# First group: low parts of the product, branch and output weights made by VectorE, those of the plain blocks by GpSimd

## The reference, cut to what matters

```
p = rms_norm(x, norm_gain) @ w_in          # columns: aq ak av ag | bq bf bi bg | ma mb
attn_o = window attention with sinks (aq, ak, av), window of two chunks of 64 tokens
rec_o  = gated linear recurrence (bq, f = lb + (1-lb)*sigmoid(bf), bi), state per head 128 x 128
ya = (attn_o * silu(ag)) @ w_branch_a
yb = (rms_norm per head(rec_o) * silu(bg)) @ w_branch_b
merged = sigmoid(ma) * ya + sigmoid(mb) * yb
y = rms_norm(x + merged @ w_out, final_norm_gain)
```

## Time and profile before

| | |
|---|---|
| runs, median (lowest to highest) | 1585.51 us (1581.87 to 1587.05), 3 runs |
| profiled execution | 1583.75 us, span 1581.8 us |
| mean granted TensorE clock | 0.989 |
| busy: PE, VectorE, ScalarE, GpSimd | 1519.4, 959.8, 537.4, 228.6 us |

### The profile page before, as it was taken

One profiled execution on the slowest core, in us unless ns is written; L12 is line 12 of the kernel. 1 busy time (PEld: TensorE's weight loads), 2 busy tenths in 40 slices (PEclk: granted clock), 3 DMA queues, 4 the chain that ended last, 5 costly groups with the idle time before them and its releaser, 6 DMA issues.

```text
span 1581.8 us, 24395 instructions
## 1 busy us (share of the span) xinstructions
PE 1519.4 (96%) x9727; PEld 1464.4 (93%) x9727; DVE 959.8 (61%) x1543; ACT 537.4 (34%) x1161; POOL 228.6 (14%) x155
## 2 busy tenths in 40 slices
PE   6999999988999799999999999999999999999996
PEld 5999899978999799999999999999989999999996
DVE  5558776973476854567777126675566758513624
ACT  5345553333413422555223110232256422210022
POOL 1422224256643400000100000100000010000000
PEclk9999999999999999999999999999999999999998
DMA  4743334378796464222226885536322233786352
GB/s 157 279 148 143 120 139 155 130 266 303 284 348 241 173 218 155 107 107 88 93 104 212 275 275 206 193 119 221 138 83 97 97 107 114 250 270 212 133 207 74
DMA packets 99136, 278.44 MB, mean 176 GB/s; under 512 B 11984, under 2 KB 29136, under 8 KB 99024
## 3 DMA queue, kind: packets, MB, share of 16 engines
q1 hardware_dynamic: 73968, 202.68, 37.6%
q10 hardware_dynamic: 25056, 74.20, 12.1%
HBM read 194.01 MB, written 82.84 MB: 175 GB/s over the span
## 4 chain that ended last, share of the span: by engine, by line
PE 81%; DVE 12%; DMA 2%; ACT 2%; issue 2%; POOL 1%; DVEq 0%; ACTq 0%
PE bank L1299 24%; PE bank L1301 23%; PE bank L1300 23%; DVE x_raw L954 2%; DMA raw<-in_w 2%; PE bank L1504 2%; PE bank L1430 1%; PE bank L1448 1%; PE bank L1500 1%; POOL w_unit L610 1%; PE bank L1486 1%; PE bank L1462 1%; PE bank L1472 1%; DVE x_acc L942 1%; PE bank L1439 1%
## 5 line engine op out<-in xcount | busy, mean ns | idle before, releaser
L1299 PE MATMUL bank<-x_hi,w_unit 128*128 128x320 f32 (+2 forms) x1680 | 556.3, 331 | 22.1 <-DVE sig L1230 9.8
L1301 PE MATMUL bank<-x_hi,w_unit 128*128 128x320 f32 (+2 forms) x1680 | 545.2, 325 | 0.0
L1300 PE MATMUL bank<-x_lo,w_unit 128*128 128x320 f32 (+2 forms) x1680 | 545.0, 324 | 0.0
L1299 PEld LDWEIGHTS bank<-x_hi,w_unit 128*128 128x128 f32 x1680 | 319.0, 190 | 33.4 <-issue 18.0
L1300 PEld LDWEIGHTS bank<-x_lo,w_unit 128*128 128x128 f32 x1680 | 319.3, 190 | 0.4
L1301 PEld LDWEIGHTS bank<-x_hi,w_unit 128*128 128x128 f32 x1680 | 318.7, 190 | 0.0
L610 POOL TENSOR_TENSOR w_unit<-w_raw,w_unit 128x512 fp32r<-128x512 f32 x102 | 145.2, 1442 | 295.4 <-ACT w_unit L657 275.4
L1299 PE MATMUL bank<-m_hi,w_unit 128*128 128x384 f32 (+1 forms) x384 | 126.3, 329 | 10.2 <-POOL w_unit L610 6.4
L1300 PE MATMUL bank<-m_lo,w_unit 128*128 128x384 f32 (+1 forms) x384 | 124.4, 324 | 0.0
L1301 PE MATMUL bank<-m_hi,w_unit 128*128 128x384 f32 (+1 forms) x384 | 124.4, 324 | 0.0
L1299 PEld LDWEIGHTS bank<-m_hi,w_unit 128*128 128x128 f32 x384 | 72.6, 189 | 13.1 <-issue 6.9
(11 more groups left out here) (206 smaller groups left out, 2608.8 us busy)
## 6 DMA issues: line engine op xcount, KB each, us to landing
w_unit<-w_parts SPq DMA_DIRECT2D x274, 512.0 KB, 4.2
w_parts<-w_unit ACTq DMA_DIRECT2D x137, 512.0 KB, 4.0
w_raw<-in_w SPq DMA_DIRECT2D x88, 256.0 KB, 3.6
res<-in_x_t SPq DMA_DIRECT2D x12, 704.0 KB, 6.9
raw<-in_w SPq DMA_DIRECT2D x28, 256.0 KB, 3.7
x_raw<-in_x_t SPq DMA_DIRECT2D x12, 384.0 KB, 8.6
out_y<-res SPq DMA_DIRECT2D x12, 384.0 KB, 5.9
x_raw<-in_x_t SPq DMA_DIRECT2D x12, 320.0 KB, 6.1
```

The source lines that it names most:

```text
L1299: pe.matmul(out, w_h, m_h, start=first, stop=False, **more)
L1300: pe.matmul(out, w_h, m_l, start=False, stop=False, **more)
L1301: return pe.matmul(out, w_l, m_h, start=False, stop=last_of_bank, **more)
```

## The change

GpSimd makes the low parts of the 56 plain units only. The other 81 are made by VectorE, from the unit `LOW_FROM` on, at places in the list of steps that a new function gives: `lows_after(step)` names the units whose low part follows a step, and they are put in behind it for group 0. In the products it is the unit four ahead, after each `prod`; ScalarE's stores go one unit further behind the high parts in the products.

```diff
--- before.py
+++ after.py
@@ -77,6 +77,7 @@
 NAMES = ([(b, i) for b in range(NP) for i in range(2)] + [(o, 0) for o in OPS]
          + [(b, i) for b in range(NP + len(MIXED), NB) for i in range(2)])
 UNITS = len(NAMES)
+LOW_FROM = 2 * NP
 PART = {n: u for u, n in enumerate(NAMES)}
 
 
@@ -114,6 +115,30 @@
 X_ALL = [step for n in X_STEPS for step in X_STEPS[n]]
 OUT = ([(j, s) for j in range(KT // 2) for s in range(2)] + [(j, s) for s in range(2) for j in range(KT // 2, KT)])
 SQUARES = len(OUT) - 2
+
+
+def lows_after(step):
+
+    kind, a, s = step
+    if kind == "evac":
+        b = BLOCK[a] + 2
+        late = a in ("av", "bf0")
+        names = [(b, i) for i in range(2) if (s == 1 if late else i == s)] if FIRST <= b < NP else []
+        names += {("ma0", 1): [(OPS[0], 0), (OPS[1], 0)], ("ma1", 1): [(OPS[2], 0), (OPS[3], 0)]}.get((a, s), [])
+    elif step == ("t_low", 3, 0):
+        names = [(OPS[4], 0)]
+    elif kind == "prod":
+        names = [(OPS[a + 4], 0)] if 1 <= a < NO - 4 else []
+        names += [(BLOCK["wab0"], i) for i in range(2) if a == NO - 2]
+    elif kind == "refill":
+        names = [(BLOCK["wab1"], i) for i in range(2)]
+    elif (kind, s) in (("ya", 1), ("yb", 0)):
+        names = [(BLOCK[f"wab{a}"] + 2, int(kind == "yb"))]
+    elif kind == "out" and a < MERGES - 2:
+        names = [(BLOCK[f"wo{a}"] + 2, i) for i in range(2) if (i == s if a < KT // 2 else s == 0)]
+    else:
+        names = []
+    return [PART[n] for n in names if PART[n] >= LOW_FROM]
 
 
 def steps(g):
@@ -191,6 +216,8 @@
             out += [("y_sum", 0, g), ("y_back", 0, g)]
     if last:
         out += [("y_sum", 1, g), ("y_back", 1, g)]
+    if g == 0:
+        out = [t for step in out for t in [step] + [("low", u, 0) for u in lows_after(step)]]
     return out
 
 
@@ -606,8 +633,8 @@
 
             u = 0, name, i
             pool.wait_ge(w_high, PART[name, i] + 1)
-            source = op_source(OP[name]) if name in OP else w_raw[PLACE[u]][:]
-            pool.tensor_tensor(low_of(u), source, high_of(u).bitcast(F32), ALU.subtract).then_inc(w_split, 1)
+            pool.tensor_tensor(low_of(u), w_raw[PLACE[u]][:], high_of(u).bitcast(F32),
+                               ALU.subtract).then_inc(w_split, 1)
 
         def x_back(dst, k, t):
 
@@ -617,7 +644,7 @@
 
         def body(g, last):
             for u, name in enumerate(NAMES):
-                if g == 0 and u >= 2 * FIRST:
+                if g == 0 and 2 * FIRST <= u < LOW_FROM:
                     low(*name)
                 if name == (BLOCK["ag0"], 1):
                     wait_read(pool, g, last, ("attend", NCH - 1, 0), 6)
@@ -665,7 +692,7 @@
             else:
                 act.wait_ge(s_made, 4 * p + (1 if op == "s3" else 4))
             act.activation(high_of((0, OPS[n], 0)), op_source(n), ACT.Copy).then_inc(w_high, 1)
-            keep_to(PART[OPS[n], 0] - 2)
+            keep_to(PART[OPS[n], 0] - 3)
 
         def prepare_x(step, g, gn, last):
             kind, s, _ = step
@@ -869,6 +896,7 @@
                 elif kind == "fetch":
                     if g == 0:
                         high(BLOCK[f"wab{a}"])
+                        keep_to(PART[BLOCK[f"wab{a}"], 0] - 2)
                 elif kind == "prod":
                     op, p = OPS[a]
                     bank = bank_of(g, step)
@@ -980,6 +1008,16 @@
             prepare_x(step, None, 0, False)
         dve.wait_ge(consts_in, 16 * 8)
         link(dve.tensor_scalar(neg_sink[:], sink[:], -1.0, None, ALU.mult))
+
+        def low(n):
+
+            name, i = NAMES[n]
+            u = 0, name, i
+            if n == LOW_FROM:
+                dve.wait_ge(w_split, LOW_FROM)
+            dve.wait_ge(w_high, n + 1)
+            source = op_source(OP[name]) if name in OP else w_raw[PLACE[u]][:]
+            dve.tensor_tensor(low_of(u), source, high_of(u).bitcast(F32), ALU.subtract).then_inc(w_split, 1)
 
         def split(hi, lo, val):
 
@@ -1240,6 +1278,8 @@
                         take(sig[:, br, j + 1, HT:T], v_sum[:], "s1")
                     else:
                         take(sig[:, br, j, HT:T], u, "s4")
+                elif kind == "low":
+                    low(a)
                 elif kind == "refill" and not last:
 
                     wait_op_done(dve, g, last, NO - 1)
```

## The result

The changed kernel takes 1586.54 us (median of 20 runs, 1584.79 to 1590.59), the kernel before 1584.47 us in the same comparison (20 runs). The ratio of the times is 1.0019, 95% interval 1.0013 to 1.0025: **slower by 2 to 4 us**, inside the 0.3% that was called no change. The forecast was 1582.1, 3.4 us under before: wrong in sign. The profiled execution of the changed kernel took 1585.42 us, 1.1 under its median, that of the kernel before 1583.75. A few executions, of whatever kernel, took 2600 to 5900 us and are left out of every time here.

A forecast was written before the change was run, and what follows sets the result against it. PE, busy 96%, was taken as the bound, so only its waits could pay. Gate products with opening -1.6 and output stage -1.8 gave -3.4 us, applied to the median 1585.51: 1582.1, range 1575.5 to 1588.5.

The forecast's parts named there:

- the two places named: PE waits in the gate products' pairs, about 10 us lost over five, and in the output stage at wo6 and wo7.
- the stretched neighbours: VectorE's two-input SBUF subtractions in the pairs, 1.57 and 1.66 us beside GpSimd, were to take 0.61 to 0.69 us.
- Opening, +3.7: Before s4 of pair 0: s1's low part stands behind `finish` on VectorE, so s4 starts about 340.6 against 336.93.
- The ring, -5.3 for five pairs: Gate products: the chain of stores, loads and parts repeating each pair was to take 14.6 us, against 15.66 before.
- the first leg: In each pair, from s2's to s4's high part, waiting for the store of a12: 4.13 us.
- the load's leg: In each pair, the load of the upper half of raw_1, up to a12's high part: 3.64 us.
- the stores and loads slow down: Rival for the pairs: same bytes in less time, store 4.5, load 4.1, ring 15.6, total 1587.0 us; chance 0.16.
- the slower rival: In the pairs, a12's late low part holds the take of s1: 16.6 us each, total 1592.0; chance 0.08.
- the last leg: In each pair, from a12's high part to the next s2's high part: 5.39 us.
- Branch projections, nothing: 16 low parts there add 0.61 us each to VectorE, hidden by PE's busy time of 7.7 us per block.
- my own signs of being wrong: s4 of pair 0 not later, period under 14 or over 15.3, or PE waiting in the branch projections.
- Output stage, -1.8: Group 0's output stage: with VectorE's work undisturbed, wo7's low part is ready at 543.6, where PE started at 545.45.

The follow-up runs named there:

- take first: The changed kernel with the low part of each pair's a12 behind the take of the pair's before s1 product, instead of ahead: 1584.85 us, ratio to before 1.0009.
- store early: The changed kernel with each product's high part again followed by the store of the unit two before it, not three: 1586.56 us, ratio to before 1.0019.
- half stores: The changed kernel with stores of the product units, and their loads in later groups, cut to the high half: 1576.59 us, ratio to before 0.9957.
- branch later: The changed kernel with the low parts of the branch projections' weights each behind a later take: 1585.78 us, ratio to before 1.0014.
- output only: The kernel before with only the low parts of the output projection's weights on VectorE, one more store at the first fetch: ratio to before 0.9993.

## Why the prediction was wrong

- **What bounds, and the prices.** Right: PE waits in the two places named, a low part costs VectorE 0.61 to 0.69 us, and the stretched neighbours went back to 0.69 (multiplications of the output stage 3.18 to 1.15).
- **Opening, +3.7.** Right in sign and mechanism, too large: +2.2. Measured from the common event the low part of s1 started at 29.35, forecast 29.4 (332.3 - 302.93). The load behind it was seen landed 2.6 us after its issue (330.61 on SP, then L1243 at 333.20), where I had taken 4.2; that is the difference. Leaving these low parts with GpSimd gives 1.4 of it back, and 1.9 to 2.1 with the take first. PE stood 4.21 us at s1 and not 6.
- **The ring, -5.3 for five pairs (-1.6 with the opening).** This is the step that failed, and with it the sign: the landing times of the transfers on the ring, above all the first leg, "store of a12: 0.03 + 4.0 to land", in all 4.13 us from s2's to s4's high part. It took 5.22 in the mean (5.64 in the pair shown), and the load's leg 3.95 for 3.64; all other legs together came 0.2 under the forecast. The 4.0 was no bad reading: a store at this place took 4.0 us before (356.90) and takes 5.5 now (355.41), with two raw loads issued 0.8 and 0.5 us ahead of it (354.57 and 354.94; before 1.8 and 0.7). The error was to carry the landing times of before into another order of transfers. Taking the same store out earlier moved the microsecond to the load (store early), and halving the bytes took 1.6 us off each pair (half stores). The rival "the stores and loads slow down" had it: a ring of 15.6, measured 15.8. I gave it 0.16, arguing that the stores would come spread out. They did (355.41 to 361.05 above, against four in 3.3 us), and that didn't help.
- **The take behind a12's low part**, the place of the slower rival, is real too, but small: 0.2 us a pair in the last leg, 0.8 to 2.8 us from s4 to s4 over the section, not 8.
- **Branch projections, nothing.** Wrong: "PE's busy time hides them" counted VectorE's work and left out that it works in order. A low part whose weights land late held a take for 5.6 us; PE waited 1.9, and the stretch from s4 of pair 6 to the first wait of the output stage took 94.42 us for 91.68 (91.85 in "branch later"). A wait of PE there was among my own signs of being wrong. This was the same head-of-line wait that I had priced for the pairs.
- **Output stage, -1.8.** Right in mechanism, and near in size: -1.5, in every kernel with these low parts on VectorE. It came mostly from the take of `res` (PE's idle behind it 1.73 to 0.68), less from wo6's own low part (4.78 to 4.42). The times of "output only" can't confirm it.

The losses of 2.2, 0.7 and 2.7, less 1.5, are the 4.2 us between the traces; that the runs show 3.0 is within what single profiles differ by. That the measured time lies in the range 1575.5 to 1588.5 comes from the range being wide: the terms of the forecast's sum missed by -1.5, +6.0, +2.7 and +0.3. What stays open is why two raw loads and two stores close together land later at the same share of the DMA engines, and how the clock's fall in "take first" would repeat.

## What to carry to other kernels

When work moves to an engine that runs in order, list what stands behind each moved instruction and what the moved instruction waits for; a cheap instruction at a late load costs its whole wait. If the loop it is taken from holds DMAs at 0.8 of their share, halve the bytes in an experiment before counting instructions: here that was worth 8 us in five pairs, while the faster engine took 2.3 us off two legs of each pair and the transfers gave it back. Read such a ring leg by leg, as means over its turns: a sum that doesn't move can hide two large changes. And split the move: the part of it behind the division, and the part at the late load, were the losses, and without them the rest gained.

## What the runs showed of the hardware

- Landing time went with what else was in flight. A store of 512 KB landed in 4.3 us in the median at 0.8 DMA share, one of 256 KB in 2.4 at 0.60; in the changed kernel, issuing stores one operation earlier raised their median to 4.8 and that of the 256 KB loads from 4.1 to 4.6. A store at the same place of the pair landed in 4.0 us before and in 5.5 in the changed kernel, where two raw loads go out closer ahead of it. In the kernel before, where no wait of ScalarE or VectorE for a store shows, halving them brought the loads' median from 3.6 to 3.2 and five pairs from 78.32 to 72.47.
- A subtraction of 128x512 with both inputs in SBUF takes VectorE 0.69 us with GpSimd idle, 1.57 and 1.66 beside it. Without the stretch the leg of the ring in which the two lie is 0.8 us shorter (6.05 to 5.26), and the pair isn't.
- After a wait of PE of 2.61 us the granted clock was 0.89 over the next 28 us; after 1.73 us at the same place it was 1.00. In the pairs it was 0.89 and 0.90 behind waits of 3.21, 2.46 (both before) and 2.34 us (changed, at 368.04), and 1.00 behind 2.16 (before, at 368.36) and 1.65 us (changed).
